# A two-layer hybrid decoder trunk: the weights' remainders of the projections by an accumulating transfer

## The reference

```python
def hybrid_layer(h, ...):
    a = rms_norm(h, attn_norm)
    proj = pad(a @ w_in)                       # one projection, split into 15 parts
    o_a = dsa_attention(...)                   # 4 heads, keys chosen by an indexer (top 128)
    o_b = forgetting_attention(...)            # 4 heads, decay by a gate
    o_c = rms_norm(gla_chunked(...), gla_out_norm) * silu(gg)   # 4 heads, linear attention
    h = h + concat(o_a, o_b, o_c) @ w_out
    f = rms_norm(h, ffn_norm)
    gate, up = split(f @ w_gate_up, 2)         # 2 x 2816 columns
    return h + (silu(gate) * up) @ w_down
```

## Time and profile before

| | |
|---|---|
| median of three runs | 1295.46 us |
| profiled execution, its own time | 1295.57 us |
| its span, first to last instruction | 1293.5 us |
| TensorE busy | 1259.0 us (97%) |
| VectorE busy | 901.5 us (70%) |
| ScalarE busy | 633.9 us (49%) |
| GpSimd busy | 439.4 us (34%) |
| granted clock of TensorE | 0.997 |
| chain that ended last | TensorE 84%, VectorE 9%, ScalarE 3%, issue 2%, DMA 1%, GpSimd 1% |
| mean transfer rate | 88 GB/s, SP's queue busy 25.2% of 16 engines |

### The profile page before, as it was taken

The page is one execution under the profiler, slowest core; times in us unless marked ns, Lnnn a source line. Parts: engine busy times, 40 slices in busy tenths (PEclk is TensorE's granted clock), DMA queues, the critical chain, the costliest instruction groups (busy, mean ns, idle before and its releaser), DMA issues.

```text
span 1293.5 us, 22962 instructions
## 1 busy us (share of the span) xinstructions
PE 1259.0 (97%) x9174; PEld 1187.0 (92%) x9174; DVE 901.5 (70%) x1520; ACT 633.9 (49%) x1016; POOL 439.4 (34%) x230
## 2 busy tenths in 40 slices
PE   7999999998999999899999999999989999999998
PEld 7989999998999999899998889988779999997887
DVE  4598898488888888722236999984888888885110
ACT  5575556655444444522235665385464445454221
POOL 2563322143222222244445453122432222214543
PEclk9999999999999999999999999999999999999999
DMA  5312211033222231222223221110322332212333
GB/s 189 94 56 83 66 34 34 34 104 115 108 99 99 99 102 63 99 98 98 97 93 101 73 77 55 50 34 24 123 98 98 112 118 99 99 66 98 99 111 115
DMA packets 27440, 113.58 MB, mean 88 GB/s; under 512 B 3664, under 2 KB 4304, under 8 KB 21968
## 3 DMA queue, kind: packets, MB, share of 16 engines
q1 hardware_dynamic: 26624, 111.18, 25.2%
q10 hardware_dynamic: 720, 1.09, 0.2%
HBM read 108.79 MB, written 2.10 MB: 86 GB/s over the span
## 4 chain that ended last, share of the span: by engine, by line
PE 84%; DVE 9%; ACT 3%; issue 2%; DMA 1%; POOL 1%; SPq 0%; DVEq 0%; ACTq 0%; POOLq 0%
PE ps L1243 21%; PE ps L857 17%; PE ps L1249 11%; PE ps L863 8%; PE ps L954 5%; PE ps L960 5%; PE ps L955 5%; PE ps L1084 2%; PE ps L1057 1%; PE ps L1067 1%; PE ps L1032 1%; DVE rstd L2041 1%; DVE score L1866 1%; DMA raw<-in_groups 1%; PE ps L1141 1%
## 5 line engine op out<-in xcount | busy, mean ns | idle before, releaser
L724 POOL TENSOR_TENSOR wlo<-raw,whi 128x1024 fp32r<-128x1024 f32 x116 | 282.9, 2440 | 477.1 <-ACT whi L1327 476.6
L1327 ACT ACTIVATE whi<-raw 128x1024 fp32r<-128x1024 f32 x116 | 122.4, 1057 | 223.8 <-PE ps L863 179.1
L954 PE MATMUL ps<-xhi,whi 128*128 128x264 f32 (+1 forms) x632 | 177.6, 310 | 0.0
L955 PE MATMUL ps<-xlo,whi 128*128 128x264 f32 (+1 forms) x632 | 171.4, 300 | 0.0
L857 PE MATMUL ps<-hhi,whi 128*128 128x264 f32 (+1 forms) x528 | 159.0, 323 | 5.2 <-DVE hlo L2105 5.2
L857 PE MATMUL ps<-hlo,whi 128*128 128x264 f32 (+1 forms) x528 | 159.0, 323 | 0.0
L954 PEld LDWEIGHTS ps<-xhi,whi 128*128 128x128 f32 x632 | 119.1, 189 | 4.5 <-issue 0.4
L955 PEld LDWEIGHTS ps<-xlo,whi 128*128 128x128 f32 x632 | 119.2, 189 | 3.9
L857 PEld LDWEIGHTS ps<-hhi,whi 128*128 128x128 f32 x528 | 100.4, 190 | 13.5 <-DVE hlo L2105 5.8
L857 PEld LDWEIGHTS ps<-hlo,whi 128*128 128x128 f32 x528 | 100.2, 190 | 7.8
L829 POOL TENSOR_TENSOR sums_a<-raw 128x1024 f32<-128x1024 f32 x22 | 53.9, 2449 | 151.4 <-PE ps L1249 151.4
(11 more groups left out here) (275 smaller groups left out, 3337.8 us busy)
## 6 DMA issues: line engine op xcount, KB each, us to landing
raw<-in_weights SPq DMA_DIRECT2D x116, 512.0 KB, 3.3
raw<-in_groups SPq DMA_DIRECT2D x42, 1024.0 KB, 4.8
out_hT<-h SPq DMA_DIRECT2D x7, 256.0 KB, 4.5
h<-in_hT SPq DMA_DIRECT2D x4, 264.0 KB, 6.5
h<-in_hT ACTq DMA_DIRECT2D x4, 264.0 KB, 6.1
cst<-in_consts SPq DMA_DIRECT2D x1, 780.5 KB, 9.4
xnb<-feat SPq DMA_DIRECT2D x20, 33.2 KB, 2.0
feat<-xnb SPq DMA_DIRECT2D x20, 33.2 KB, 2.0
```

The costliest lines, as they stand in the source:

```text
L724: nc.gpsimd.tensor_tensor(wlo[:, b], raw[:, b], whi[:, b].bitcast(F32), ALU.subtract).then_inc(split_done, 1)
L954: nc.tensor.matmul(o, whi[:, k % 2, n], xhi[:, n, cut], start=(n == 0), stop=False)
L955: nc.tensor.matmul(o, whi[:, k % 2, n], xlo[:, n, cut], start=False, stop=False)
L1327: return nc.scalar.activation(whi[:, b], raw[:, b], ACT.Copy).then_inc(hi_done, 1)
```

## The change

For the first 34 units of each layer GpSimd no longer subtracts. ScalarE writes the negated rounded tile into `wlo` (`negate_slot`, a copy with scale -1 that reads `raw`), which releases the new semaphore `neg_done`; GpSimd then issues a transfer of the same unit from HBM that adds onto `wlo` (`add_unit`, `accum_op=ALU.add`), and its landing releases `added[b]`, one semaphore for each buffer, on which the low pass now waits. The negation stands ahead of the rounding, but behind it in units 0 and 1. SP loads the next raw tile once both copies were made. The 24 units of the down projection are split as before. Where GpSimd's clearing steps waited for its own last split, they now wait for its last split of squares, if there was one.

```diff
@@ -610,6 +613,14 @@
         def fox_q(hd):
             return q_odd[:, hd // 2] if hd % 2 else feat[:, place(FQ + hd // 2)]
 
+        def added_to(l, n):
+
+            return added[n % 2], 16 * (l * (N_ADDED // 2) + n // 2 + 1)
+
+        def split_to(l, n):
+
+            return split_done, l * N_SPLIT + n - U_DN + 1
+
         def group_slot(n):
 
             if n % 2:
@@ -634,7 +645,13 @@
         def _(sp):
             def load_unit(n, b):
 
-                sp.wait_ge(split_done, n + 1)
+                if n >= 2:
+                    of, at = divmod(n - 2, UNITS)
+                    if at < U_DN:
+                        sp.wait_ge(hi_done, n - 1)
+                        sp.wait_ge(neg_done, of * N_ADDED + at + 1)
+                    else:
+                        sp.wait_ge(*split_to(of, at))
                 sp.dma_start(raw[:, b].rearrange("p k n -> p (k n)"), weights[n]).then_inc(raw_loaded[b], 16)
 
             def load_h(k):
@@ -717,20 +734,23 @@
 
         @block.gpsimd
         def _(pool):
-            pool.sem_inc(split_done, 2)
-
             def split_unit(n, b):
                 pool.wait_ge(hi_done, n + 1)
                 nc.gpsimd.tensor_tensor(wlo[:, b], raw[:, b], whi[:, b].bitcast(F32),
                                         ALU.subtract).then_inc(split_done, 1)
 
+            def add_unit(n):
+
+                of, at = divmod(n, UNITS)
+                pool.wait_ge(neg_done, of * N_ADDED + at + 1)
+                pool.dma_start(wlo[:, at % 2].rearrange("p k n -> p (k n)"), weights[n], accum_op=ALU.add).then_inc(added[at % 2], 16)
+
             for l in range(DEPTH):
                 ev, g0 = layer[l], l * GROUPS_7
-                split, zeroed = [2 + l * UNITS], [0]
+                zeroed, squared = [0], [0]
 
                 def proj(k, hf, p):
-                    split_unit(l * UNITS + k + 2, k % 2)
-                    split[0] += 1
+                    add_unit(l * UNITS + k + 2)
 
                 def cleared(ins):
                     zeroed[0] += 1
@@ -747,7 +767,8 @@
                     if l:
                         pool.wait_ge(half_done, 4 + 2 * l * UNITS)
                     pool.wait_ge(cst_loaded, 16)
-                    pool.wait_ge(split_done, 2 + split[0])
+                    if squared[0]:
+                        pool.wait_ge(ev.sq_split, squared[0])
                     nc.gpsimd.memset(lr_parts[:].bitcast(F32), 0.0).then_inc(ev.masks_ready, 1)
                     nc.gpsimd.memset(causal16[:, 0:NT - QB], 0.0).then_inc(ev.masks_ready, 1)
                     pool.wait_ge(ev.masks_ready, 2)
...
@@ -806,17 +832,18 @@
                     pool.wait_ge(ev.sq_whole, SPLIT_SQUARES.index(k) + 1)
                     pool.wait_ge(ev.sq_ready, SQUARES[k] + 1)
                     nc.gpsimd.tensor_tensor(sq_parts[:, 0], sqb[:, 0], sq_parts[:, 1].bitcast(F32), ALU.subtract).then_inc(ev.sq_split, 1)
+                    squared[0] += 1
 
                 do = dict(proj=proj, square_parts=square, masks=masks, clear_fox=clear_fox, spread_sums=spread_sums, clear_even=clear_even,
                           clear_gla_even=clear_gla_even, clear_gla_odd=clear_gla_odd)
                 for b in range(2):
                     if l == 0:
-                        split_unit(b, b)
+                        add_unit(b)
                 for step in ORDER[l][POOLE]:
                     do[step[0]](*step[1:])
 
                 for n in range(N_PROJ + 2, U_DN):
-                    split_unit(l * UNITS + n, n % 2)
+                    add_unit(l * UNITS + n)
 
                 for n in range(1, GROUPS_7 + 1):
                     raw_blocks, _, sums, _, _ = group_slot(n)
@@ -829,8 +856,11 @@
                     nc.gpsimd.tensor_tensor(sums[:, SUM_P:SUM_V + 1], raw_blocks[:, RAW_B11:RAW_B22 + 1], b21,
                                             ALU.add).then_inc(sv.pv_summed, 1)
 
-                for n in range(U_DN, UNITS + (2 if l < DEPTH - 1 else 0)):
+                for n in range(U_DN, UNITS):
                     split_unit(l * UNITS + n, n % 2)
+                if l < DEPTH - 1:
+                    for b in range(2):
+                        add_unit((l + 1) * UNITS + b)
 
 
         @block.tensor
@@ -873,7 +903,7 @@
                             pe.wait_ge(*w)
                         high_pass(n, b, bank_no, parts[hf], x, (k,), first and k == order[0])
                     if hf == 0:
-                        pe.wait_ge(split_done, l * UNITS + (n + 3))
+                        pe.wait_ge(*low_ready)
                     low_pass(n, b, bank_no, parts[hf], x, order, last).then_inc(half_done, 2 // len(parts))
 
                 def x_tiles(k):
...
@@ -955,7 +985,7 @@
                             nc.tensor.matmul(o, whi[:, k % 2, n], xlo[:, n, cut], start=False, stop=False)
                         return
                     if begins:
-                        pe.wait_ge(split_done, l * UNITS + (k + 3))
+                        pe.wait_ge(*added_to(l, k))
                     for n in range(KT):
                         ins = nc.tensor.matmul(o, wlo[:, k % 2, n], xhi[:, n, cut], start=False, stop=(n == KT - 1))
                     ins.then_inc(half_done, 2 if proj_first(l, k) else 1)
...
@@ -1326,6 +1356,9 @@
             def round_slot(b):
                 return nc.scalar.activation(whi[:, b], raw[:, b], ACT.Copy).then_inc(hi_done, 1)
 
+            def negate_slot(b):
+                nc.scalar.activation(wlo[:, b], raw[:, b], ACT.Copy, scale=-1.0).then_inc(neg_done, 1)
+
 
             act.wait_ge(gain_loaded, 16)
             for k in range(KT):
@@ -1334,6 +1367,7 @@
                 if k in (0, 5):
                     act.wait_ge(raw_loaded[k // 5], 16)
                     round_slot(k // 5)
+                    negate_slot(k // 5)
                 if k % 2 == 0:
                     if k >= 4:
                         act.wait_ge(h_done, k - 3)
@@ -1349,6 +1383,8 @@
 
                     act.wait_ge(half_done, n * 2 + (half0 - 2))
                     act.wait_ge(raw_loaded[slot], (n - slot) * 8 + (raw0 + 16))
+                    if n % UNITS < U_DN:
+                        negate_slot(slot)
                     round_slot(slot)
 
                 def chain(ins):
```

More of the change, by code:

```diff
@@ L40 @@
 STREAM = DEPTH * UNITS
+N_ADDED, N_SPLIT = U_DN, UNITS - U_DN
 DN_PARTS = (8, 8, 6)
@@ L533, in hybrid_block @@
         hi_done = sem("hi_done")
+        neg_done = sem("neg_done")
+        added = [sem("added0"), sem("added1")]
         split_done = sem("split_done")
@@ L865, in low_pass, with unit_part @@
                     return ins
-                def unit_part(b, n, bank_no, hf, parts, x, order=range(KT), first=True, last=True, waits={}):
+                def unit_part(b, n, low_ready, bank_no, hf, parts, x, order=range(KT), first=True, last=True, waits={}):
                     if hf == 0:
@@ L1168, in out @@
                         pe.wait_ge(hi_done, l * UNITS + (U_OUT + part + 1))
-                        pe.wait_ge(split_done, l * UNITS + (U_OUT + part + 3))
+                        pe.wait_ge(*added_to(l, U_OUT + part))
                         for n, hf in early:
@@ L1205, in _ @@
                         for hf in range(len(parts)):
-                            unit_part(b, j * 2 + (U_OUT + b), 2 * b + hf, hf, parts, mix_tiles)
+                            unit_part(b, j * 2 + (U_OUT + b), (added[b], j * 16 + 16 * (l * (N_ADDED // 2) + U_OUT // 2 + 1)), 2 * b + hf, hf, parts, mix_tiles)
                 for ks in (range(KT - 1), (KT - 1,)):
@@ L1297, in _ @@
                         for hf in range(len(parts)):
-                            unit_part(b, U_DN + 2 * s + b, 2 * b + hf, hf, parts, hidden_tiles, order=range(k0, k0 + kts),
+                            unit_part(b, U_DN + 2 * s + b, split_to(l, U_DN + 2 * s + b), 2 * b + hf, hf, parts, hidden_tiles, order=range(k0, k0 + kts),
                                       first=(s == 0), last=(s == 2),
@@ L1307, in _ @@
                             for hf in range(len(parts)):
-                                unit_part((3 * b + s) % 2, j * 6 + (U_DN + 3 * b + s), 2 * b + hf, hf, parts, hidden_tiles,
+                                unit_part((3 * b + s) % 2, j * 6 + (U_DN + 3 * b + s), (split_done, j * 6 + (l * N_SPLIT + 3 * b + s + 1)), 2 * b + hf, hf, parts, hidden_tiles,
                                           order=range(k0, k0 + kts), first=(s == 0), last=(s == 2))
```

7 lines of the change are left out of this document (4 added, 3 removed).

## The result

The changed kernel takes 1329.06 us (median of four runs, 1324.35 to 1329.8) against 1295.4 for the kernel before: a ratio of 1.0254, 95% interval 1.0229 to 1.0278. The forecast was 1310 with a range of 1291 to 1360. The direction and the place are as forecast, the loss is 33.7 us in place of 14.5.

What follows compares the result with a forecast made beforehand. TensorE's string of matmuls was taken to bound the kernel: 1295.6 us + 21 of waits for late transfers + 1 for copies - 7.8 from VectorE gave 1309.8, said as 1310 us, range 1291 to 1360.

Steps and rivals of the forecast that it cites:

- What bounds the kernel: TensorE, busy 1259.0 of 1293.5 us: any added matmul wait counts almost in full, relief elsewhere returns at most the holes.
- all four units named: Low passes of layer 0's unit 17 and layer 1's 11, 14, 26 would wait 2 to 3 us each for the transfer.
- D: Time from the end of ScalarE's negation to the accumulating transfer's landing: 6.3 us, with ends 3.3 and 9.4.
- The table of slacks: Per-unit spare time before the low pass; stalls are D less slack less the previous stall, summing to 21 us.
- VectorE's gain: VectorE freed from GpSimd's subtractions: 4.9 us in layer 1's output projection, 0.9 in layer 0's, 2 in mixers; 7.8 together.
- The copies: ScalarE's 68 negations, mostly covered by the other buffer's matmuls: 1 us lost, between 0 and 4.
- A: Rival, faster: the accumulating transfer is hardly dearer than a plain load, D at most 4.4, 1292 us; chance 0.15.
- B in its first form: Rival, no effect: D between 4.4 and 5.1, about 1296 us; chance 0.10 for both forms.
- B's second form: Rival, no effect: VectorE's gain near 13 us against about 13 lost at D = 5.5; chance 0.10 for both forms.
- C: Rival, much slower: the accumulation itself is the bound, D of 8 to 9.4 and beyond, 1341 to 1370 us; chance 0.22.
- over 7 is C: Sign in the profile after: GpSimd's transfers taking over 7 us to land would mean C.
- the forecast's case: D from 5.1 to 7.5, ending between 1298 and 1331 us; chance 0.53.

Runs made afterwards that it cites:

- e3: Changed kernel with SP loading the next raw tile only once the addition has landed: 1325.31 us.
- e11: Changed kernel with each accumulating transfer carrying only the first half of its unit (256 KB), the other half staying negated: 1295.32 us.
- e1: Changed kernel without the accumulating transfer; the low pass waits for the negation and reads only the negated rounded tile: 1286.87 us.
- e2: Changed kernel with a plain load of the same 512 KB over the negated tile, without the addition: 1288.64 us.
- e12: Kernel before with only layer 1's units 27 to 33 by accumulating transfer, raw tiles loaded early: 1291.17 us.
- e7: Kernel before with ScalarE's 68 negations added, overwritten by GpSimd's subtraction, and TensorE's output-projection loop written out: 1305.83 us.
- e9: Kernel before with only TensorE's output-projection loop over units 26 to 31 written out, as control: 1295.65 us.
- e4: Changed kernel with ScalarE rounding first and negating second, so the transfer starts 1.04 us later: 1366.13 us.

## Why the prediction was right and wrong

- **What bounds the kernel, and where the loss comes: right.** TensorE waits for the transfer, and all four units named wait: layer 0's 17 (3.48, the longest of all), layer 1's 26 (2.39), 11 (1.93) and, with less than the 2 to 3 us named, 14 (0.90). Layer 1's 15 (3.40) and layer 0's 26 (3.32) are as long and were not named. Layer 0's 27 to 31 hardly wait, but for 31 (2.16), where the first load of a group runs beside the transfer and the prediction had only a raw tile beside it (that this is the cause was not tested apart). The plain loads were not what TensorE waited for.
- **D: this is the step that failed.** I took 4.8 + 1.5 = 6.3 us and it is 7.3. Of its parts, "twice the bytes" was good (3.0 to 3.1 us of engine time, against 1.5 for SP's plain load), and the raw load beside it as well (1.6 for 1.5). Missing were about 0.5 of the fixed part (an estimated 2.3 where SP's load has 1.8, e3 and e11) and the 0.3 to 0.4 before GpSimd begins to issue, which stood in no row. The page "DMA: Bandwidth & Descriptors" of the Trainium skill, section "Latency and other measured facts", which I cited for 6.7, was nearer: a later first byte from GpSimd is what the traces show (first packet after 1.6 us, or 1.25 without the addition, against SP's 0.96), with the time before the issue on top. What the page "SBUF — State Buffer" of the Trainium skill says in "SBUF: two separate sides" is hardly tested here: the 68 issues take 0.86 to 0.90 us, one 1.02, and only two of VectorE's instructions of the kinds that it names ran beside one, `tensor_scalar` both times, with the issue at 0.87 and 0.88.
- **The table of slacks: right in form.** On e1 as zero it gives 4 us at D = 4.3 (e2: 1.8 measured), 16 at 5.8 (e11: 8.4) and 38 at 7.3 (the changed kernel: 42.2). For the waits alone it is too high throughout: 1.5, 11.2 and 28.3 us are measured. For the time it is too high at small D and too low at 7.3, where its sum leaves out TensorE's longer busy time. The forecast had 21 us of loss, and it is 42.2: 7.3 more of waits, 11.4 of busy time, and 2.5 between these two and the difference of the medians.
- **TensorE's clock: not foreseen.** This is the second term that failed: the sum had stalls only and nothing for the clock. Five of the long waits have stretches of lower clock with them, and the busy time rose by 11.4 us over e1, an estimated 6.8 of it by the clock.
- **VectorE's gain: right at the output projections, wrong in the mixers.** Layer 1's stage gains 3.4 with 1.5 of a new wait in it (e12), which is the 4.9 of the forecast; layer 0's gains 0.9 in e1, as said. In the mixers e1 gains 5.2 us and the copies take 4.5 + 2.6 there (e7 against e9), so the relief is worth some 12 if the two add up, where I took 2 and at most 6.9: I had counted TensorE's holes in four windows only.
- **The copies: wrong.** 10.2 us for 1. That they were covered unit by unit was argued from the plain stretches; 7.1 us of the loss lie in the mixers, where ScalarE's other work stands behind the copies, but the path of most of it is open. If they add up, the two errors, +9 and -10, cancelled by luck, and the net gain of 8.1, near the forecast's 6.8, hides both.
- **The rivals.** A, and B in its first form, needed D below 5.1; e2, at 4.3, shows that A's D holds for a transfer that doesn't add. B's second form had a loss of about 13 us, and it is 42.2. C named the accumulation as the cause, and "over 7 is C" was its sign: at 7.0 the landing is on the border, while the time, 1329, is still in the forecast's case (1298 to 1331), at its upper end.

## What to carry to other kernels

Before a remainder or a sum is moved into an accumulating transfer, read for each tile the time from the last write to the first reader, compare it with the landing (here 7 us), and ask as well what the engine that it relieves was holding up: at seven tiles, with 6.3 us of slack and more, in a stage where TensorE waited for VectorE, it gained 3.9 us; at 49 tiles it was even, as the copies cost too; at 68 it lost 33.7. Where a table of slacks is steep (e4: 37 us for one microsecond), the forecast is only as good as the latency, so measure that by itself first. And an engine that is half busy is not free of charge: price extra copies by a run that adds only them (here 10.2 us for 68).

## What the hardware showed that I had not expected

- An accumulating transfer from HBM takes 3.0 us of all 16 engines for 512 KB, a plain one from the same queue 1.8; it lands after 5.4 us alone, 7.0 with a 512 KB load issued 0.6 us behind it, 7.7 with one issued 0.3 us ahead of it (e3, the changed kernel, e4), 8.3 in the one case with a 1024 KB load 0.86 us behind it. These are medians but for the last; single landings in the changed kernel range from 5.2 to 8.8. The plain one, with the load behind it, lands after 4.0 (e2).
- Its issue holds GpSimd for 0.88 us; the plain one's for 0.54.
- Some of the waits of 1.9 to 3.5 us in a TensorE that is otherwise full cost more than themselves: a granted clock of 0.57 to 0.83 in windows of 4 us at five of eight such waits, 1.00 at the other three.
